# Eight U rows and sixteen dots in a tile of the picking, and fourteen U rows left for the end

## The reference, cut to what matters

```
s = einsum('phcd,hckd->phck', qy, sub_keys)      # scores of 2 x 128 keys
top_s, top_i = top_k(s, 16)
best_s, best_j = top_k(sums of the two halves, 16)
gate = softmax(best_s)
act = gelu(einsum('pd,phkd->phk', xb, expert_u[experts]))
out = einsum('phk,phkd->pd', gate * act, expert_v[experts])
```

## Time and profile before

| | us |
|---|---|
| median of three runs | 3510.15 (3505.91 to 3510.48) |
| the profiled execution's own time | 3515.87 |
| its span | 3513.9 |
| PE busy | 3350.1 (95%) |
| DVE busy | 2484.5 (71%) |
| ACT busy | 1170.5 (33%) |
| POOL busy | 809.0 (23%) |
| mean granted clock of PE | 0.977 |

### The profile page before, as it was taken

One profiled execution on the slowest core, in us unless ns is written; L12 is line 12 of the kernel. 1 busy time (PEld: TensorE's weight loads), 2 busy tenths in 40 slices (PEclk: granted clock), 3 DMA queues, 4 the chain that ended last, 5 costly groups with the idle time before them and its releaser, 6 DMA issues. The chain is left out here.

```text
span 3513.9 us, 53612 instructions
## 1 busy us (share of the span) xinstructions
PE 3350.1 (95%) x18867; PEld 3067.8 (87%) x18867; DVE 2484.5 (71%) x5064; ACT 1170.5 (33%) x2011; POOL 809.0 (23%) x908
## 2 busy tenths in 40 slices
PE   5998999989799999999999999999999999999998
PEld 4997998968688899999999999998788888888886
DVE  6545777544678768888888886613777777777777
ACT  3002566442322223225666664222222222222220
POOL 1000111011000013433333333501333333333331
PEclk8998999989899999999999999999999999999999
DMA  6622222154211147667888888854999899998996
GB/s 255 229 101 85 92 85 85 43 180 129 104 41 53 65 152 242 232 223 260 296 295 301 304 299 305 294 160 138 290 292 292 282 293 285 287 293 280 291 293 237
DMA packets 426022, 743.20 MB, mean 212 GB/s; under 512 B 224945, under 2 KB 276321, under 8 KB 416609
## 3 DMA queue, kind: packets, MB, share of 16 engines
q0 software_dynamic: 99200, 371.24, 31.4%
q1 hardware_dynamic: 318048, 316.89, 28.7%
q10 hardware_dynamic: 8576, 52.47, 3.8%
HBM read 607.30 MB, written 133.19 MB: 211 GB/s over the span
## 5 line engine op out<-in xcount | busy, mean ns | idle before, releaser
L477 PE MATMUL apab<-h2hi,auhib 128*128 128x384 f32 x2048 | 704.5, 344 | 17.1 <-DVEq L61 13.8
L479 PE MATMUL apab<-h2hi,aulob 128*128 128x384 f32 x2048 | 687.6, 336 | 0.0
L478 PE MATMUL apab<-h2lo,auhib 128*128 128x384 f32 x2048 | 687.5, 336 | 0.0
L1520 POOL DMA_INDIRECT nx<-in_expert_v,fw_now x256 | 315.3, 1232 | 698.3 <-DVE acc L1546 680.2
L477 PEld LDWEIGHTS apab<-h2hi,auhib 128*128 128x128 f32 x2048 | 387.5, 189 | 19.5 <-DVEq L61 15.6
L478 PEld LDWEIGHTS apab<-h2lo,auhib 128*128 128x128 f32 x2048 | 387.4, 189 | 0.0
L479 PEld LDWEIGHTS apab<-h2hi,aulob 128*128 128x128 f32 x2048 | 386.2, 189 | 0.0
L1546 DVE SCALAR_TENSOR_TENSOR acc<-nx,fw_share,acc 128x1024 f32<-128x1024 f32 x256 | 327.2, 1278 | 0.5 <-DVE raw L2399 0.5
L2462 PE MATMUL eheld<-vhi,Hhi 128*128 128x512 f32 x768 | 303.2, 395 | 6.4 <-SPq L2322 3.9
L2462 PE MATMUL evo<-vhi,Hhi 128*128 128x512 f32 x768 | 301.7, 393 | 6.7 <-DVEq L61 4.6
L1602 DVE TENSOR_TENSOR aulob<-raw,auhib 128x1024 fp32r<-128x1024 f32 x128 | 156.6, 1224 | 213.7 <-ACT auhib L1598 213.1
(11 more groups left out here) (335 smaller groups left out, 7314.4 us busy)
## 6 DMA issues: line engine op xcount, KB each, us to landing
raw<-in_expert_u POOLq DMA_DIRECT2D x128, 512.0 KB, 5.5
raw<-in_expert_v SPq DMA_DIRECT2D x124, 512.0 KB, 3.9
ahead_dram<-ageb SPq DMA_DIRECT2D x256, 192.0 KB, 4.0
gates_dram<-arena ACTq DMA_DIRECT2D x48, 1024.0 KB, 6.1
urow<-ahead_dram SPq DMA_DIRECT2D x128, 384.0 KB, 5.8
ijw<-gates_dram SPq DMA_DIRECT2D x96, 384.0 KB, 7.3
late<-in_w_ada SPq DMA_DIRECT2D x48, 512.0 KB, 5.6
left<-gates_dram SPq DMA_DIRECT2D x32, 384.0 KB, 8.1
```

Of the source, the lines that this page charges most:

```text
L477: pe.matmul(out, lhi, rhi, start=(k == 0), stop=False)
L478: pe.matmul(out, lhi, rlo, start=False, stop=False)
L479: return pe.matmul(out, llo, rhi, start=False, stop=(k == n - 1))
L1520: pool.indirect_dma_start(self.ring[i], None, table, bass.IndirectOffsetOnAxis(ap=self.now[:, h, i:i + 1], axis=0)).then_inc(self.row_in[i ...
```

## The change

A tile takes eight U rows and 16 items instead of six and 12, and its DVE work is in eight parts instead of six. With eight tiles 16 more U rows are done in that stage, and `ROW_REST` becomes 114. Twenty-four more items are used there, so 16 are left for the last rows instead of 40: `WITH` is 2 instead of 5. The last U rows are 14 instead of 30, in 7 turns, and `PREPARE` is 2 instead of 10. The loads of the first V rows stand in turn 1 (`PREPARE - 1`), all four in its second half, behind the gathers and a wait for all items. SP's store loop ends after two rows (`at` = 116 as before, now R+2 instead of R+18).

```
-ROWS_TILE = 6
-DOTS_TO = [1, 2, 3, 5, 9, 12]
+ROWS_TILE = 8
+DOTS_TO = [2, 3, 5, 7, 9, 11, 14, 16]
 ROWS_BLOCK = 4
-TILE_BATCHES = 3
+TILE_BATCHES = 4
@@ rows_phase
-    assert PREPARE > WITH
+    assert PREPARE >= WITH
@@ gpsimd, rest_rows
-                        if turn == PREPARE - 1:
+                        if turn == PREPARE - 1 and p:
                             pool.wait_ge(few.row_used.sem, few.row_used.done(ITEMS - 1))
-                            for q in range(p * VQ // 2, (p + 1) * VQ // 2):
+                            for q in range(VQ):
                                 pool.dma_start(V.first[q], expert_v[q * P:(q + 1) * P, :]).then_inc(v_first[q], 16)
@@ vector, tile
-                    dots(0)
+                    dots(0, 1)
                     cut(0)
@@
+                    dots(2)
+                    cut(1)
@@
-                    dots(1)
-                    cut(1)
-
                     link(dve.tensor_copy(lists.rearrange("p c a h -> p h c a"), tl(TI)))
                     if not (sparse or first):
                         turned(t + (-1), at + (-1))
+                    dots(3, 4)
+                    cut(2)
+
                     look_up(0)
-                    dots(2)
-                    cut(2)
+                    dots(5, 6)
+                    cut(3)
 
                     look_up(1)
-                    dots(3, 4)
-                    cut(3)
-
-                    dots(5, 6)
+                    dots(7, 8)
+                    cut(4)
+
                     dve.wait_ge(be_done, t + 1)
@@
-                    dots(7, 8)
-                    cut(4)
-                    dots(9, 10, 11)
+                    dots(9, 10)
                     cut(5)
+                    dots(11, 12, 13)
+                    cut(6)
+                    dots(14, 15)
+                    cut(7)
```

## The result

The changed kernel took 3525.8 us (median of 20 runs), the kernel before 3511.16 us (median of 20). The ratio is 1.0037 with a 95% interval of 1.0021 to 1.0053: slower, by about 13 us.

What follows compares the result with a forecast made beforehand. PE, busy for 95% of the span, was taken to bound the kernel. Behind R+3 it would lose 23.6 us (stall 21.3, clock 2.3) instead of 11.1: +12.5 us on the median of 3510.15, so 3523 us, range 3513 to 3533.

Steps and rivals of the forecast that it cites:

- More rows in the tiles cost 0 and gain 0: Tiles: 133.1 us of rows move there from the end; PE has no wait to fill, so cost and gain are 0.
- R+0 to R+3 keep their waits: First two turns of the last rows: PE's waits ahead of these rows stay, 2.72 us with them.
- When the last dot ends: Last rows: the sixteenth dot ends at 2220.5 instead of 2216.8, 3.7 us later for the gates loads; bounds 2216.8 and 2225.0.
- From there to the gelu: Last rows: from the last dot to the gelu of R+3 takes 6.9 us; bounds 2.7 and 9.95.
- rival 3: Last rows: a second stall, or the store behind 2 MB of V rows, 5.7 us more; over 3533 us, chance 0.06.
- The stall: Ahead of R+4: PE waits 21.3 us, as stores stand behind SP's wait for all items; bounds 13.4 and 28.9.
- The clock behind it: After the stall ahead of R+4: PE's lower clock adds 2.3 us; bounds 1.5 and 4.2.
- The load of R+6 is hidden by the stall: Last rows: POOL's later load for R+6 lands by some 2233, before R+6 starts at 2246.9; otherwise a second wait shows.
- The sum: Behind R+3: 23.6 us lost instead of 11.1, so +12.5 us; +3.8 with all lower bounds, +22.0 with all upper.
- the first (SP is not held): Last rows: gelus of R+3 meet their bank, so -6.5 us, 3504 us; chance 0.13.
- The second, a short stall: Last rows: gathers lose nothing to gates loads, stores land quickly; +3.8 to +7 us, 3514 to 3517; chance 0.12.
- The fourth, cuts that come late in the tiles: Six dense tiles: the cut behind the exponentials misses its margin by 1 us each, 6 us on top, 3529; chance 0.04.

Runs made afterwards that it cites:

- e3: The kernel before, six rows and twelve items in a tile, with the preparation put right behind the last turn with items; 3523.65 us, ratio 1.0034.
- e1: The changed kernel with SP's stores of R+2 and R+3 issued before its wait for all items; 3512.19 us, ratio 0.9994 to the kernel before.
- e2: The kernel before with SP's stores of R+18 and R+19 issued ahead of the two ahead_first loads; 3504.25 us, ratio 0.998.
- e7: The changed kernel with SP's gates loads spread between stores, stores of R+2 and R+3 ahead of the wait for all items; 3522.68 us, ratio 1.002.
- e9: The changed kernel with SP's order as in e7, and POOL's V rows moved behind the loads of R+6 and R+7; 3502.61 us, ratio 0.9958.
- e4: The changed kernel with the four gates loads issued behind the stores of R+2 and R+3 instead of before the wait for all items; 3517.33 us, ratio 1.0023.
- e5: The changed kernel with POOL's wait for all items and V-row loads moved from turn 1 to the second half of turn 2; 3533.21 us, ratio 1.0049.
- e8: The kernel before with the same spread order on SP as e7; 3513.63 us, ratio 1.0004.
- e10: The same edit as e8 to the kernel before, made once more; 3510.29 us, ratio 0.9988.

## Why the prediction was right

3523 us and a range of 3513 to 3533 were forecast; 3525.8 was measured. By its own steps:

- *More rows in the tiles cost 0 and gain 0.* The part up to the first block differs by 133.2 us for 133.1 us of rows. Right. e3 shows the loss without any change to a tile. (The margin behind the exponentials comes out of its rows as 1.2 us, not 1.1.)
- *R+0 to R+3 keep their waits.* 1.24 and 2.21 us ahead of R+2 and R+3, for 1.48 and 2.72. The stretch from the first block to R+3 is still 3.3 us longer, which the sum did not have. R+3 took 9.84 us (2327.36 to 2337.20) for 8.28 before (2198.21 to 2206.49), at a granted clock of 0.83, and the first eight matmuls of the blocks 2.08 us for 1.16. The two cost 2.8 us and 1.6, and the shorter waits give some of it back. Both follow a wait of PE; why the clock fell behind these and not behind the like waits of the old trace isn't settled. The 2.08 us come in e1, e2, e7 and e9 too, the 1.16 in e3, e4, e5, e8 and e10, so this is no doing of the larger tile. The slow R+3 comes in e1, e5 and e9 too, and in no kernel with the small tile; the kernel before has its slow start a row later, in R+4 (6.12 us for 4.55, as the prediction read). Whether the tile has a part in that is open.
- *When the last dot ends.* +3.7 us were forecast, +0.3 measured. The single terms were better than their sum: the gates loads do cost 3.75 us (e4), and without them, with the stores held back, the dots end 3.4 us sooner than before (26.52 for 29.95), where I had put 8.2 against 4.5. The kernel before's 29.95 is the highest of five like profiles (e4 above), so both the 0.3 and the 3.4 have an uncertainty of some 3 us.
- *From there to the gelu.* 6.9 us were forecast, 8.8 measured: SP's issue was free as assumed (0.82 us for two loads), and the landing took longer. 3.2 us of the 8.8 are the V rows, with perhaps the load for R+6 (e5). The rule of queues taken in turn, from the Trainium skill (DMA: Bandwidth & Descriptors, "Queues, rings and completion order"), that I set against rival 3 left a cost, if a smaller one than the 5.7 us.
- *The stall.* 21.3 us forecast, 18.87 measured (2337.20 + 0.17 to 2356.24). The last dot's term takes 3.4 off, the landing adds 1.9, and R+3 ended 1.0 us later against the start of R+2 than before (20.66 us for 19.63), which shortens the stall by as much.
- *The clock behind it.* 2.3 us forecast, 7.23 - 4.55 = 2.7 measured (2356.24 to 2363.47).
- *The load of R+6 is hidden by the stall, and would show as a second wait if it weren't.* Right in both halves: no wait there in the changed kernel, 3.53 us in e7, 0.30 in e9.
- *The sum.* +12.5 us forecast behind R+3, +10.6 measured, and 3.3 ahead of it that were not in the sum: 14.0 by the profile. The whole times say 13 to 15. The mechanism is the one forecast. That the number came within 3 us is in part luck: the terms were off by 3.4, 1.9 and 1.0 us in ways that largely cancel, and the 3.3 us ahead of R+3 are clock that the sum did not have.

Of the rivals, the first (SP is not held) is ruled out by SP's wait of 12.3 us. The second, a short stall, held neither in the stall nor in the sum, though its first half, dots that hardly end later, came close (+0.3 us). The third was to be over 3533: its V rows cost up to 3.2 of the 5.7 us, and its second wait came only once the first was gone (e7). The fourth, cuts that come late in the tiles, did not show: PE has no wait there. One step of the reasoning was too narrow, and e1 shows it: I took the wait for the items as the only thing that holds the stores. Without it 6.3 of the 18.7 us stay, for SP's issue of four gates loads takes 12.6 us (14.2 in the changed kernel). With these spread out as well 2.68 us are left (e7), the wait for the lower cut, so some 3.7 of the 6.3 are the gates loads'.

## What to carry to other kernels

An in-order queue that issues loads for the next stage and stores for this one couples the two: ask of every wait in it what stands behind it, and how many steps lie between the wait and the event it waits for. Work that "only moves" can take that distance away, at no cost in the stage it moves to. Put stores whose buffer is single ahead of such a wait, and transfers of many small pieces between stores rather than in a row; and when a stall is gone, look at once for the next transfer that it had been hiding. Here the exchange of two steps took 13 us of the changed kernel's stretch away (e1). The spread order took 7.5 us off the kernel before's stretch (e8, e10), and its whole time is not shown to be shorter for it.

## What the runs showed of the hardware that I had not expected

- Four loads of 384 KB in pieces of 64 floats kept SP's queue for 14.2 us in the changed kernel (2320.31 to 2334.55), 12.6 in e1, 13.3 in e5 and 17.4 in e3, each time beside the gathers; without gathers they took 7.5 us of issue, 7.2 in e2 and 6.8 in e4. The sends of gates had landed each time, in e3 long before.
- A wait of PE of 2.87 us ahead of the first block, behind a stage in which PE never stopped, was followed by eight matmuls in 1.16 us in six of eleven profiled executions and in 2.08 us in five, where the block's start took 2.8 us more.
- Code that no kernel here changes took up to 20 us more or less from one profiled execution to another (first tile at 1192.1 to 1211.9), four times the 4.5 us that e9 gains in its stretch. From the expert stage's first matmul to the end of the span it took 1067.9 to 1075.8 us.
